# One matmul per 128-token block instead of four 32-wide ones in levels -1 to 4 of an HGRN2 attention

## The reference, cut to what matters

```python
def hgrn2_mixer(x, w_in, lower_bound, hgrn_norm_g, w_out):
    q_raw, f_raw, i_in, z = jnp.split(x @ w_in, 4, axis=-1)
    f = lower_bound + (1.0 - lower_bound) * jax.nn.sigmoid(f_raw)
    q, k, logf = jax.nn.silu(q_raw), 1.0 - f, jnp.log(f)
    # S_t = diag(f_t) S_{t-1} + k_t v_t^T,   o_t = S_t^T q_t
    o = hgrn2_recurrence(heads(q), heads(k), heads(i_in), heads(logf))
    o = rms_norm(o, hgrn_norm_g) * jax.nn.silu(heads(z))
    return o.reshape(bsz, s, HGRN_WIDTH) @ w_out
```

## Time and profile before

| | |
|---|---|
| median of three runs | 1356.23 us |
| lowest, highest run | 1351.24, 1356.72 us |
| the profiled execution: its own time, span | 1356.72 us, 1354.5 us |
| TensorE matmul busy | 1303.1 us (96%) |
| VectorE busy | 956.5 us (71%) |
| ScalarE busy | 740.1 us (55%) |
| mean granted TensorE clock | 0.982 |

### The profile page before, as it was taken

How to read it: one execution, slowest core, us unless ns; L and a number is a source line. 1 busy time by engine, 2 the same in 40 slices (tenths; PEclk the granted TensorE clock), 3 DMA queues, 4 the chain that set the end, 5 groups by cost and what they waited for, 6 DMA issues and landing times.

```text
span 1354.5 us, 30017 instructions
## 1 busy us (share of the span) xinstructions
PE 1303.1 (96%) x13136; PEld 1190.6 (88%) x13136; DVE 956.5 (71%) x1504; ACT 740.1 (55%) x995; POOL 25.5 (2%) x59
## 2 busy tenths in 40 slices
PE   6998899999999999999899998999999999999998
PEld 5998789899999999998898777988889898988887
DVE  4877857556468888888545895988767675797543
ACT  6676344436555565565345235777435884687531
POOL 0000000000000000000000000000000000000000
PEclk9999889989999999999899998999999999999999
DMA  6545453445267555655123324488775333466551
GB/s 262 187 162 212 188 188 118 153 162 184 97 237 267 218 214 188 215 203 207 64 94 124 126 96 187 159 297 293 293 264 185 125 125 126 187 248 210 194 187 63
DMA packets 34658, 247.51 MB, mean 183 GB/s; under 512 B 3872, under 2 KB 3872, under 8 KB 4960
## 3 DMA queue, kind: packets, MB, share of 16 engines
q1 hardware_dynamic: 29392, 209.16, 42.3%
q0 software_dynamic: 5136, 36.44, 7.4%
HBM read 244.53 MB, written 1.05 MB: 181 GB/s over the span
## 4 chain that ended last, share of the span: by engine, by line
PE 84%; DVE 7%; ACT 5%; issue 3%; DMA 0%; DVEq 0%; ACTq 0%
PE PS L499 15%; PE PS L419 10%; PE PS L420 9%; PE PS L421 9%; PE PS L500 7%; PE PS L514 7%; DVE WL L587 3%; ACT WH L574 2%; PE PS L435 2%; PE PS L436 2%; PE PS L437 2%; PE PS L1018 2%; PE PS L957 1%; PE PS L458 1%; DVE BIG L299 1%
## 5 line engine op out<-in xcount | busy, mean ns | idle before, releaser
L587 DVE TENSOR_TENSOR WL<-RAW,WH 128x2048 fp32r<-128x2048 f32 x166 | 380.1, 2290 | 112.4 <-ACT WH L574 108.9
L574 ACT ACTIVATE WH<-RAW 128x2048 fp32r<-128x2048 f32 x166 | 316.9, 1909 | 174.3 <-PE PS L500 70.0
L419 PE MATMUL PS<-XW,WH 128*128 128x256 f32 x992 | 292.9, 295 | 12.4 <-DVE WL L587 12.4
L420 PE MATMUL PS<-XW,WH 128*128 128x256 f32 x992 | 284.0, 286 | 0.0
L421 PE MATMUL PS<-XW,WL 128*128 128x256 f32 x992 | 283.7, 286 | 0.0
L419 PEld LDWEIGHTS PS<-XW,WH 128*128 128x128 f32 x992 | 193.4, 195 | 16.3 <-DVE WL L587 12.4
L420 PEld LDWEIGHTS PS<-XW,WH 128*128 128x128 f32 x992 | 193.8, 195 | 0.4 <-issue 0.2
L421 PEld LDWEIGHTS PS<-XW,WL 128*128 128x128 f32 x992 | 193.5, 195 | 0.0
L499 PE MATMUL PS<-XW,WH 128*128 128x512 f32 x392 | 141.1, 399 | 0.2
L299 DVE SCALAR_TENSOR_TENSOR BIG<-BIG,C 128x256 f32<-128x256 f32 (+2 forms) x228 | 101.4, 507 | 32.8 <-ACT BIG L1379 13.5
L500 PE MATMUL PS<-XW,WL 128*128 128x256 f32 x392 | 110.0, 281 | 0.0
(11 more groups left out here) (400 smaller groups left out, 2563.8 us busy)
## 6 DMA issues: line engine op xcount, KB each, us to landing
RAW<-wst SPq DMA_DIRECT2D x196, 1024.0 KB, 4.8
BIG<-wad POOLq DMA_DIRECT2D x34, 1024.0 KB, 5.1
X<-xT SPq DMA_DIRECT2D x1, 1024.0 KB, 4.8
outT<-X SPq DMA_DIRECT2D x4, 256.0 KB, 4.2
K<-cst SPq DMA_DIRECT2D x1, 608.0 KB
CB<-crow SPq DMA_DIRECT2D x1, 512.0 KB
BIG<-pT POOLq DMA_DIRECT2D x2, 256.0 KB, 3.8
C<-cols SPq DMA_DIRECT2D x1, 370.0 KB
```

The costliest lines, as they stand in the source:

```text
L419: pe.matmul(o, h, hl[0][:, k0 + k, :], start=(k == 0), stop=False)
L420: pe.matmul(o, h, hl[1][:, k0 + k, :], start=False, stop=False)
L574: ac.activation(WH[p % NS][:, :], RAW[u % NR][:, :], ACT.Copy).then_inc(S.hi.tick(p), 1)
L587: ve.tensor_tensor(WL[p % NS][:, :], RAW[u % NR][:, :], WH[p % NS][:, :].bitcast(f32), ALU.subtract).then_inc(S.lo.tick(p), 1)
```

## The change

Levels -1 to 4 use the whole 128-token block as weights. Level -1: four matmuls of 128 weight columns and 128 moving columns. Levels 0 to 4: four matmuls of 128 weight columns and 64 moving columns, the 64 tokens of the block that lie in odd blocks of 2^lv. The four strips of each block go. The wanted entries lie in the bank where they lay, and their readers are unchanged; the other entries of the bank are written too, and masked away as before. The new condition `0 <= lv < 7` names levels 5 and 6 too, but the branches `if lv == 5` and `elif lv == 6` stand ahead of it and are kept, so that these levels, like level 7, stay as they are.

```diff
+        def by_blocks(x, w):
+            return x.rearrange("p m (c b i s) -> p (m c) b i s", c=2, i=2, s=w)
...
                 for m in range(4):
                     c = 128 * (m % 2)
                     t = pe.matmul(PS[b][0:64, 64 * m:64 * m + 64], k[:, m // 2, c:c + 64], q[:, m // 2, c + 64:c + 128], start=True, stop=True)
-            elif lv < 5:
+            elif 0 <= lv < 7:
+                qs = by_blocks(q, 1 << lv)
                 for m in range(4):
-                    for a in range(0, 128, 32):
-                        r = slice(128 * (m % 2) + a, 128 * (m % 2) + a + 32)
-                        if lv < 0:
-                            o, qs = PS[b][a:a + 32, 128 * m + a:128 * m + a + 32], q[:, m // 2, r]
-                        else:
-                            o = PS[b][a:a + 32, 64 * m + a // 2:64 * m + a // 2 + 16]
-                            qs = q[:, m // 2, r].rearrange("p (b i s) -> p b i s", i=2, s=1 << lv)[:, :, 1, :]
-                        t = pe.matmul(o, k[:, m // 2, r], qs, start=True, stop=True)
+                    t = pe.matmul(PS[b][:, m * 64:(m + 1) * 64], k[:, m // 2, blk(m % 2)], qs[:, m, :, 1, :], start=True, stop=True)
+            elif lv < 0:
+                for m in range(4):
+                    t = pe.matmul(PS[b][:, blk(m)], k[:, m // 2, blk(m % 2)], q[:, m // 2, blk(m % 2)], start=True, stop=True)
             else:
                 for m in range(2):
                     t = pe.matmul(PS[b][:, blk(m)], k[:, m, 0:128], q[:, m, 128:256], start=True, stop=True)
```

## The result

The changed kernel is slower, as forecast: 1369.8 us median of four runs (1363.8 to 1373.57) against 1354.03 (four runs of the kernel before, 1351.24 to 1356.72), ratio 1.0112 with a 95% interval of 1.0066 to 1.0158. Two later timings of the same two kernels gave 1.0153 (1.013 to 1.0177) and 1.0099 (1.0062 to 1.0135). The difference is small but clear of the noise in each of the three. The forecast was 1371 us and 1.011 (1371.0/1356.23). That the medians come within 1.2 us of each other is partly luck: the base of the forecast was 2.2 us above the later median of the kernel before, and the change cost 15.8 us where 14.8 had been forecast.

A forecast was written before the change was run, and what follows sets the result against it. TensorE's stream was taken to bound seven of eight pairs. Seven pairs at +1.84 us (+12.9) and the last at +1.2 gave +14.1 us on 1356.72, so 1371 us; range of 8 in 10: 1362 to 1378 us.

The forecast's parts named there:

- TensorE's stream bounds the layer: HGRN2 layer, seven of eight pairs of heads: TensorE covered at full clock, so its gains or losses are the kernel's.
- A level costs 0.57 us, level -1 0.59 us: Price before the change in TensorE's stream of projection matmuls; for level 1, 0.37 us of records plus 0.19 on both sides.
- Level -1 afterwards 0.88 us, +0.29: Level -1 after the change: eight records of 0.11 us, 0.88 us against 0.59 before.
- Levels 0 to 4 load-bound, 0.88 us, +0.31: Levels 0 to 4 after the change: the 128-column weight load sets 0.11 us a record, +0.31 us a level.
- A pair +1.84 us: One pair of heads: level -1's +0.29 plus five levels at +0.31 us; levels 5 to 7 unchanged.
- The last pair +1.2 us, levels 1 and 3 hidden: Last pair: levels -1, 0, 2 and 4 add 0.29 + 3 x 0.31 us; TensorE's waits cover levels 1 and 3.
- The sum +14.1 us: Whole kernel: seven pairs +12.9 us and the last +1.2 us, on the profiled execution of 1356.72 us.
- B (moving-bound): Levels 0 to 4: moving columns set the pace, each 0.14 us cheaper; eight pairs -3.3 us, 1353 us; chance 0.05.
- C (76 ns a record): Levels 0 to 4: record distance stays at level 6's 76 ns, +0.04 us a level; 1361 us; chance 0.08.
- D (load and edge don't overlap, 134 ns): Levels 0 to 4: 134 ns a record at 128 columns, +0.50 us a level; 1379 us; chance 0.07.
- E (hidden): Pairs: levels lengthen, but something else sets the pace and takes back over half; 1363 us or less; chance 0.04.
- A: Main case, load-bound levels: 1371 us, with clock spread of some 3.5 us either way, 1367 to 1375; chance 0.73.

The follow-up runs named there:

- each part alone: Block form for level -1 only (1356.31 us, ratio 1.0021) or levels 0 to 4 only (1373.81 us, 1.0158), the other part in strips as in the kernel before.
- 32 and 128 moving columns: Changed kernel with 32 or 128 instead of 64 moving columns in levels 0 to 4: 1372.06 and 1373.73 us; a pair 32.35 us in both.
- blocks twice: Changed kernel with the block matmuls of levels 0 to 4 issued twice in a row into the same place: 1408.94 us, a pair 36.82 us.
- doubling the strips: Kernel before with the strip matmuls of levels 0 to 4 issued twice in a row into the same place: 1369.62 us, a pair 31.94 us.

## Why the prediction was right

- **TensorE's stream bounds the layer; what a level gains or loses, seven pairs lose.** Right for seven pairs. The layer's windows stay covered at clock 1.00. The edits whose price had been measured before (each part alone, 32 and 128 moving columns, blocks twice) came out to 0.02 us a level; those whose price was extrapolated missed by 0.02 to 0.15.
- **A level costs 0.57 us, level -1 0.59 us.** Right as sums. Their split wasn't: I took 0.37 us of records and 0.19 of edges, and doubling the strips gives 0.29 and 0.28. The 47 and 76 ns a record hold part of the edge too.
- **Level -1 afterwards 0.88 us, +0.29.** Measured 0.90, +0.31 alone.
- **Levels 0 to 4 load-bound, 0.88 us, +0.31.** This was the step without a row. Measured 0.89, +0.32. It is load-bound for the stated reason: moving 32, 64 or 128 columns changes nothing, loading 96 columns takes a record from 0.111 to 0.087 us, and four, two and one file for the same 1024 columns cost 0.57, 0.78 and 0.89 us. The two pages of the Trainium skill pointed opposite ways. The edge of the one (TensorEngine Tiling (Array Packing), Key Properties) is real in size, 0.28 us by the doubled strips, larger than the 0.19 us I read; that it is a drain no run here shows. It is outweighed by the load of the other (TensorE: Matmul & The Clock Gate, LDWEIGHTS (loading the stationary operand)). Estimates by that section's rule, 107 ns for 128 columns and 80 for 96, stand against 111 and 87 measured.
- **A pair +1.84 us.** Measured +1.93, 5% more, from the two roundings above.
- **The last pair +1.2 us, levels 1 and 3 hidden.** The mechanism held: the waits ahead of levels 2 and 4 shrank by 0.3 us each, one level's growth. The size can't be read from two profiles, since half-clock time moves that pair by 3 us from run to run. From level 7 of pair 6 to the end the mean of the profiles grew by 2.6 us (728.2 to 730.8), not 1.2: the prediction took the clock's part as a spread to either side, and the traces lean to the slow one.
- **The sum +14.1 us.** With the measured pairs 7 x 1.93 + 1.2 = 14.7 us; 14.9 us at equal clock, 16.2 as the plain means of all runs. The three medians differ by 12 to 20 us, which is the clock's scatter on both sides.
- **The rivals.** B (moving-bound) fell by the runs with 32 and 128 columns, C (76 ns a record) by the 0.111 us measured, D (load and edge don't overlap, 134 ns) by the same, E (hidden) by the pairs. The clock spread that A was given, 3.5 us either way, roughly fits the three medians of the change (1366.4 to 1372.5 us) but not single executions (1360.9 to 1376.5). The recorded chance of no difference, 0.15, is 0.02 under what C, E and B sum to.
- **Signs named beforehand.** 384 records in all at 8 a level, no wait in pairs 0 to 6, 192 ns loads and 32.3 us a pair came as said. Two signs misled. The matmul starts lie 0.101 us apart, and it is their loads that lie 0.111 apart. And L420 was to follow L419 by 0.12 us, but follows by 0.20. The lag of a matmul behind its load explains both: it is 0.11 us at the level's start (444.35 and 444.46), 0.03 us at L419 (445.24 and 445.27) and 0.11 us again at L420. That isn't an edge, as the doubled blocks show: eight more records cost 0.89 us.

## What to carry to other kernels

Count what a small matmul loads, not only what it multiplies: up to 128 moving columns over 128 weight columns, a record of this kernel cost its weight load, and loading 128 columns in one file takes longer than loading the same number in four column strips side by side, even with the edges paid. Fewer instructions in a trace are no gain in themselves (1152 fewer here, and about 15 us more). For an effect of one per cent in a kernel whose time scatters by half of one either way, measure a stretch of the trace that runs at full clock without waits; it gave 1.93 us a pair where the whole times gave 12 to 20 us in all. But a stretch chosen so leaves out what happens elsewhere, here the clock at the end of the layer and the stops without a releaser; look at the whole time as well.

## What the runs showed of the hardware that wasn't expected

- In the full tile form the starts of eight matmuls with 128 weight columns and 32 to 128 moving ones lie 0.81 us apart in sum, while their loads take 0.89; the difference shows between the first and second matmul of the next group. Matmul starts alone understate a load-bound group.
- In column strips a record took 47 ns with 32 weight columns and 16 or 32 moving, 71 ns with 32 and 64, 74 ns with 64 and 32, 76 ns with 64 and 64: neither the load alone nor the larger of the two. In longer trains it fell to 36 ns with 32 and 16 (0.29 us for the second 32 records in four strips).
- These start distances hold part of the edge. An estimate that takes 0.28 us of edges off the whole cost of each such level gives 36 ns (32 weight columns; 16 or 32 moving), 62 (64, 32), 65 (64, 64) and 61 (32, 64). With the 87 and 111 ns of 96 and 128 weight columns in the full form, the series 36, 62, 87, 111 rises by 24 to 26 ns for every 32 weight columns, in strips as in the full form. It rests on the edge being the same for all strips, which no run shows.
- Going from the projections' full form into strips and back costs about 0.28 us, once per group of strips, by the doubled strips. Groups of 96 weight columns show no such edge: eight records of 0.087 us are the whole 0.70 us.
